# Seven products of quarters in both layers' channel mixers, token sums on GpSimd, and other ring slots ahead of attention

## The reference

```python
def swiglu(h, wg, wu, wd):
    return (jax.nn.silu(h @ wg) * (h @ wu)) @ wd

def block_tail(...):
    ...
    x = x + g1[:, None, :] * rmsnorm(mixed, n_post_mix)
    hf = modulate(rmsnorm(x, n_pre_ffn), sh2, sc2)
    return x + g2[:, None, :] * rmsnorm(swiglu(hf, w_ffn_gate, w_ffn_up, w_ffn_down), n_post_ffn)
```

## Time and profile before

| what | before |
|---|---|
| median of 3 runs | 2259.72 us (2258.64 to 2261.53) |
| the profiled execution's own time | 2261.28 us |
| its span in the trace | 2259.5 us |
| PE busy | 2172.2 us, 96% of the span |
| DVE busy | 1421.0 us, 63% |
| ACT busy | 884.2 us, 39% |
| POOL busy | 107.5 us, 5% |
| mean granted TensorE clock | 0.987 |
| weight loads (raw<-w_main) | 276 of 512 KB, 3.7 us from issue to landing |

### The profile page before, as it was taken

One profiled execution on the slowest core, in us unless ns is written; L12 is line 12 of the kernel. 1 busy time (PEld: TensorE's weight loads), 2 busy tenths in 40 slices (PEclk: granted clock), 3 DMA queues, 4 the chain that ended last, 5 costly groups with the idle time before them and its releaser, 6 DMA issues.

```text
span 2259.5 us, 34079 instructions
## 1 busy us (share of the span) xinstructions
PE 2172.2 (96%) x14296; PEld 2061.5 (91%) x14296; DVE 1421.0 (63%) x2226; ACT 884.2 (39%) x1417; POOL 107.5 (5%) x199
## 2 busy tenths in 40 slices
PE   5999999899999999999979999999999999999997
PEld 3999999899979899999969999999999798999996
DVE  5587765377747543343375777674765557878785
ACT  4644432376334221221265544324763434332332
POOL 1000011010000000000000000001100000000000
PEclk9999999999999999999999999999999999999998
DMA  6333244123335212222204332443233512222223
GB/s 273 98 112 113 88 162 139 64 93 144 115 98 190 102 66 84 75 66 67 97 11 149 112 113 89 160 148 103 87 112 70 180 59 66 76 93 75 94 75 131
DMA packets 61785, 239.92 MB, mean 106 GB/s; under 512 B 7936, under 2 KB 7968, under 8 KB 59200
## 3 DMA queue, kind: packets, MB, share of 16 engines
q1 hardware_dynamic: 41040, 153.12, 20.7%
q0 software_dynamic: 20592, 84.62, 10.7%
HBM read 226.67 MB, written 11.04 MB: 105 GB/s over the span
## 4 chain that ended last, share of the span: by engine, by line
PE 86%; DVE 6%; ACT 3%; DMA 3%; issue 1%; DVEq 1%; ACTq 0%; POOL 0%; SPq 0%; POOLq 0%
PE unit L473 12%; PE unit L474 12%; PE unit L476 12%; PE unit L461 11%; PE unit L462 11%; PE unit L463 11%; PE sc L463 2%; PE sc L462 2%; PE sc L461 2%; DVE junk L1593 2%; DMA raw<-w_main 2%; PE tp L463 2%; PE tp L461 2%; PE tp L462 2%; PE tp L738 1%
## 5 line engine op out<-in xcount | busy, mean ns | idle before, releaser
L473 PE MATMUL unit<-hmh,wh 128*128 128x320 f32 x1728 | 520.9, 309 | 2.0 <-DVE vl L1503 1.2
L474 PE MATMUL unit<-hml,wh 128*128 128x320 f32 x1728 | 520.8, 310 | 0.0
L1493 DVE TENSOR_TENSOR wl<-raw,wh 128x1024 fp32r<-128x1024 f32 x240 | 291.1, 1222 | 258.0 <-ACT wh L1073 253.0
L476 PE MATMUL unit<-hmh,wl 128*128 128x320 f32 x1728 | 394.1, 309 | 0.0
L473 PEld LDWEIGHTS unit<-hmh,wh 128*128 128x128 f32 x1728 | 324.3, 188 | 3.9 <-issue 2.9
L474 PEld LDWEIGHTS unit<-hml,wh 128*128 128x128 f32 x1728 | 324.6, 188 | 1.1
L1073 ACT ACTIVATE wh<-raw 128x1024 fp32r<-128x1024 f32 x240 | 246.8, 1050 | 130.7 <-DMA raw<-w_main 130.4
L476 PEld LDWEIGHTS unit<-hmh,wl 128*128 128x128 f32 x1728 | 289.0, 188 | 0.0
L1593 DVE CUSTOM_DVE_ANT_0 junk<-ada,csb,par 128x1024 f32<-128x1024 f32 x160 | 205.6, 1285 | 23.1 <-DMA ada<-w_ada 2.6
L461 PE MATMUL unit<-wh,hmh 128*128 128x256 f32 (+1 forms) x640 | 201.9, 315 | 16.0 <-DVE nv L1503 8.8
L462 PE MATMUL unit<-wl,hmh 128*128 128x256 f32 (+1 forms) x640 | 200.1, 313 | 0.0
(11 more groups left out here) (436 smaller groups left out, 4210.3 us busy)
## 6 DMA issues: line engine op xcount, KB each, us to landing
raw<-w_main SPq DMA_DIRECT2D x276, 512.0 KB, 3.7
ada<-w_ada POOLq DMA_DIRECT2D x80, 512.0 KB, 4.2
first<-w_first SPq DMA_DIRECT2D x8, 1024.0 KB, 19.0
bias<-biases POOLq DMA_DIRECT2D x32, 192.0 KB, 2.7
x<-x POOLq DMA_DIRECT2D x2, 2560.0 KB, 12.1
x<-x_keep POOLq DMA_DIRECT2D x2, 2560.0 KB, 10.5
bias<-biases POOLq DMA_DIRECT2D x16, 256.0 KB, 3.9
gains<-g_rows POOLq DMA_DIRECT2D x4, 1024.0 KB, 5.4
```

The costliest lines, as they stand in the source:

```text
L473: pe.matmul(u[:, h, 0:n], a[0], xs[h][0], start=f, stop=False)
L474: pe.matmul(u[:, h, 0:n], a[0], xs[h][1], start=False, stop=False)
L476: mm = pe.matmul(u[:, h, 0:n], a[1], xs[h][0], start=False, stop=z)
L1493: dve.tensor_tensor(wl[slot[i]][:, :], raw[slot[i]][:, :], f32(wh[slot[i]][:, :]), ALU.subtract)\
```

## The change

It has these parts.

1. Blocks 2 to 10 of the first layer's channel mixer take seven products too; all conditions on the last layer go, and semaphore counts get an offset per layer. The slabs of the first layer's gate and up are stored in the other order that `seven` wants.
2. With that the first layer gets what only the last had: x is stored to x_keep by tiles and loaded back before the layer's end, the ring has six slots from slab 76 on, block 1 has its two splits less, ACT copies its first down tiles, the gains are loaded late. New is that POOL loads rel, pos and rope again after the last seven products (`constants_of_heads`), and that DVE and ACT wait for it at the second layer's start.
3. t1w, t2w and t4w are made by POOL in both layers (`token_sum`), not by DVE.
4. Since t4 destroys csb, the ada pieces of blocks 0 and 1 fall from 10 to 6, all in block 0. Two more pieces go to the first head after head 0 in each layer, two others to the gates.
5. `TURNED` fixes the slots of slabs 39, 40 and 41 of each layer, and 42 and 43 are held to slots 0 and 1.
6. Small moves: ACT takes the silu of csb one copy earlier; at the first layer's end the split of slab 140 moves from tile 4 to behind the last tile.

```diff
+TURNED = {39: 0, 40: 3, 41: 2, PER_LAYER + 39: 1, PER_LAYER + 40: 2, PER_LAYER + 41: 3}
-HEADS_ADA, LAST_ADA = 15, 32
+HEADS_ADA, LAST_ADA = 17, 32
...
-            may = range(SIX) if i // PER_LAYER == DEPTH - 1 and j >= 4 + W_O + KD else range(2) if NARROW <= j < WIDE else range(2, RING) if NARROW - 2 <= j < NARROW else range(RING) if j < WIDE or LAST <= j < LAST + 4 else range(RING, RING + MORE) if j >= LAST - 2 else range(RING + MORE)
+            may = (TURNED[i],) if i in TURNED else range(SIX) if j >= 4 + W_O + KD else range(2) if NARROW - 4 <= j < NARROW - 2 or NARROW <= j < WIDE else range(2, RING) if NARROW - 2 <= j < NARROW else range(RING) if j < WIDE else range(RING + MORE)
...
                 def gate_up(b):
-                    if l < DEPTH - 1 or b < SEVEN:
+                    if b < SEVEN:
                         for _ in range(4):
                             column()
...
+            def constants_of_heads():
+                for to, of in ((rel[:, :], rel_in), (pos[:, :, :], pos_in), (rope[:, :, :], rope_in)):
+                    g.dma_start(to, of).then_inc(const_in, 16)
...
+            def token_sum(n, a, b, more):
+
+                to = whole_sums[n]
+                g.tensor_tensor(to, a, b, ALU.subtract).then_inc(ts_step, 1)
+                token_steps.add()
+                for other, op in more:
+                    g.wait_ge(ts_step, token_steps.count)
+                    i = g.tensor_tensor(to, to, other, op)
...
-                    modulation(10)
+                    modulation(4)
+                token_sum(0, h12, h11, ((l12, ALU.add), (l11, ALU.subtract)))
+                if l == 0:
+                    modulation(2)
+                g.wait_ge(ts_full, 4 * l + 1)
+                token_sum(1, h22, whole_sums[0], ((l22, ALU.add),))
+                if l == 0:
                     g.wait_ge(ada_done, FIRST_ADA)
+                g.wait_ge(ts_full, 4 * l + 2)
+                token_sum(3, h21, whole_sums[1], ((l21, ALU.add),))
+                last_gate = (l + 1) * SEVENS - 2
+                g.wait_ge(seven_done, 7 * (last_gate + 1))
                 gains_on_all(1)
-                if l == DEPTH - 1:
-
-                    g.wait_ge(seven_done, 7 * (last_gate + 1) + 3)
-                    g.dma_start(x[:, :, :], x_keep).then_inc(x_back, 16)
+                g.wait_ge(seven_done, 7 * (last_gate + 1) + 3)
+                g.dma_start(x[:, :, :], x_keep).then_inc(x_back, 16)
+                if l < DEPTH - 1:
+                    g.wait_ge(seven_done, 7 * (l + 1) * SEVENS)
+                    constants_of_heads()
...
-                        elif n == 0:
-                            sum_of_tokens(0)
-                            sum_of_tokens(1)
-                        else:
+                        elif n:
                             low_of_tokens((3,))
                         if l == 0:
-                            modulation((1, 3)[n] if b == 0 else (2, 2)[n] if b == 1 else 0)
+                            modulation(3 if b == 0 else 0)
...
-                if l == DEPTH - 1:
-                    dve.wait_ge(x_back, (l + 3) * 16)
+                dve.wait_ge(x_back, (2 * l + 3) * 16)
```

More of the change, by code:

```diff
@@ L442, in build @@
         slab_done = []
+        h11, h12, h21, h22 = (f32(hmh[:, k:k + 4, h * HALF:h * HALF + HALF]) for k in (0, 4) for h in range(2))
+        l11, l12, l21, l22 = (f32(hml[:, k:k + 4, h * HALF:h * HALF + HALF]) for k in (0, 4) for h in range(2))
         FIRST_ADA = DEPTH * ADA - 2 * KD - LAST_ADA
@@ L879, in seven @@
                     pe.wait_ge(ws_ready, r + 1)
-                    pe.wait_ge(ts_ready, 2)
+                    pe.wait_ge(ts_ready, 4 * l + 2)
                     if r:
@@ L890, in seven @@
                     pe.wait_ge(w_lo[slot[i + 1]], turn_of[i + 1])
-                    pe.wait_ge(ts_ready, 4)
+                    pe.wait_ge(ts_ready, 4 * l + 4)
                     pe.wait_ge(seven_copied, r + 1)
@@ L977, in modulation @@
                     adas.add()
+            token_steps = Tally()
+            def token_sum(n, a, b, more):
[5 more added lines that the diff above has]
+                    i = g.tensor_tensor(to, to, other, op)
+                    if other is more[-1][0]:
+                        i.then_inc(ts_full, 1)
+                    else:
+                        i.then_inc(ts_step, 1)
+                        token_steps.add()
             for l in range(DEPTH):
@@ L1207, in _ @@
                     U.release(act.activation(y[:, 4, :], u[:, 0, 0:DV], ACT.Copy))
-                    u = U.get()
-                    U.release(act.activation(y[:, 0:4, :], u[:, :, :].rearrange("p a (b n) -> p (a b) n", b=2), ACT.Copy))
                     if h == 0:
@@ L1212, in _ @@
                         act.activation(csb[:, :, :], csb[:, :, :], ACT.Silu).then_inc(cs_ready, 1)
+                    u = U.get()
+                    U.release(act.activation(y[:, 0:4, :], u[:, :, :].rearrange("p a (b n) -> p (a b) n", b=2), ACT.Copy))
                     heads.add()
@@ L1414, in seven_copy @@
                 def seven_copy(r):
+                    r += l * SEVENS
                     act.wait_ge(seven_done, 7 * r + 1)
@@ L1462, in _ @@
                         U.add(TILES)
-                        if l < DEPTH - 1:
-                            split(2)
                 act.activation(flag_a[:, :], epsc[:, :], ACT.Sqrt)
@@ L1478, in _ @@
                         root(x[:, t, :], mix[:, t, :], ss2, rt2, t)
-                    if l == 0 and t in (2, 3, 4):
+                    if l == 0 and t in (2, 3, 5):
                         split()
@@ L1638, in head_norm @@
                 if h == 0 and layer.count:
-                    dve.wait_ge(x_saved, layer.count * 16)
+                    dve.wait_ge(x_saved, layer.count * (TILES + 1) * 16)
                 gain = [par[:, layer.count, GN + h * 2 + c:GN + h * 2 + c + 1] for c in range(2)]
@@ L1790, in _ @@
                         if c < 3 or j == 0:
-                            modulation(1)
+                            modulation(2 if l == 0 and j and c == 1 else 1)
                 dve.drain()
@@ L2149, in main_slabs @@
     gate_up = [np.concatenate([slabs_of(w[:, b * 256:(b + 1) * 256], P)[[i]] for i in range(2) for w in (w_fg, w_fu)]) for b in range(FB)]
-    if last:
-        for b in range(SEVEN, FB):
-            gate_up[b] = gate_up[b][[0, 2, 1, 3]]
+    for b in range(SEVEN, FB):
+        gate_up[b] = gate_up[b][[0, 2, 1, 3]]
     down = [slabs_of(w_fd[b * 256:(b + 1) * 256], 512, 2) for b in range(FB)]
```

123 lines of the change are left out of this document (47 added, 76 removed).

## The result

The changed kernel takes 2233.07 us, median of four runs (2231.71 to 2235.8), against 2260.62 us (2258.64 to 2261.76) of the kernel before on the same chip: a ratio of 0.9882, 95% interval 0.9868 to 0.9897. It is faster by 27.5 us; I had forecast 41, and the measured time lies 3.6 us outside my range. The profiled execution took 2232.49 us, its span is 2230.7.

A forecast was written before the change was run, and what follows sets the result against it. PE, busy for 96% of the span, was taken as the bound. 33.48 + 10.31 - 2.74 = 41.05 us off the profiled 2261.28 gave 2220.2, or 2218.7 us as median, range 2214.5 to 2229.5.

The forecast's parts named there:

- Seven products in layer 1: Blocks 2 to 10 of layer 1 fall from 363.90 to 330.42 us, as in layer 2: 33.48 us less.
- Slots ahead of attention: The two `values` ahead of attention in layer 1 fall from 39.40 to 29.09 us: 10.31 us less.
- The wait of 4.1 us ahead of down(0) in both layers: PE's 4.12 us wait stays in layer 2 and comes to layer 1, whose blocks 0 and 1 take 2.74 us more.
- Ada pieces: Block 0 of layer 1: three pieces ahead of the first multiply instead of one, 4.6 us of cover, cost 0.
- POOL's seven adds: Token sums in both layers: 3 us per add, 21 in all, hidden behind eight columns of PE, cost 0.
- GpSimd holds DVE: Rival, chance 0.11: in layer 1 POOL's adds stop DVE for 10.4 us, 5.8 reach PE, giving 2224.5 us.
- My own sign of being wrong: The forecast is wrong if, among other signs, DVE's ada pieces grow beyond 1.28 us each by more than a third.
- The clock: Waits of a few us may find the lower clock (0.97 and 0.95 in blocks 0 and 1): 3 us either side.
- The head of layer 2: The moved silu and moved split are as in layer 2 or stand where an engine waits: cost 0.
- x comes back late: Rival, chance 0.07: x's load at layer 1's end is 2.8 us late, 2221.5 us; with the tables up to 15.
- the wait only moves: Rival, chance 0.05: ahead of attention in layer 1 the 10.3 us are not gained, giving 2229.0 us.
- a far slower GpSimd: Rival, chance 0.04: PE's second quarter waits for token sums; at 12 us per add 80 us are lost, 2298.5.

The follow-up runs named there:

- experiment 4: The changed kernel with the down pair's second slab split ahead of block 1's last multiply, on ACT and DVE, both layers: 2215.64 us.
- experiment 1: The changed kernel with the seven adds of token sums back on DVE instead of POOL, in both layers: 2224.49 us.
- experiment 6: The changed kernel with ACT waiting for the three tables in layer 1 alone and the split back at t = 4: 2235.29 us.

## Why the prediction was right and wrong

*Seven products in layer 1: right.* 33.47 us for 33.48. *Slots ahead of attention: right* in layer 1 (10.33 for 10.31); slabs 39 and 41 were in time. That layer 2 needed them as well I had not seen; it cost nothing, since the change holds both layers. *The wait of 4.1 us ahead of down(0) in both layers: right*, and for the reason given; experiment 4 took it away.

*Ada pieces: wrong, in "PE needs the unit at 718.38: 4.6 us of cover, cost 0".* I took the first multiply's reader one column too late. In the changed kernel PE stops 14.4 us behind the mixer's start (698.16 after 683.78); put into the trace of before that is 711.4, when the multiply was over at 708.13. So 3.2 us were free, where I reckoned with 10.2 (4.6 after the pieces), and 5.6 us of pieces overdraw them: 2.4 by this, 2.6 measured (experiment 1).

*POOL's seven adds: the price was right, "the sums are hidden behind eight columns of PE: 0" was not.* The sums are ready when ACT comes for them, but they hold DVE. The rival was in the text (GpSimd holds DVE, chance 0.11) with 5.8 us on PE; 7.4 are measured. I worked its size from DVE's rate for the adds, 10.4 us. What counts is the add of POOL that a DVE instruction meets, 2.97 us and not 1.49: the holds sum to 12.5 us in layer 1, 7.4 of them ahead of the first multiply (and to 10.8 in layer 2, where PE waits for none of them). And I let 4.6 us of cover stand against it, which with the right deadline are not there. My own sign of being wrong came true: ada instructions grew from 1.28 to 3.8 us, far beyond a third. The Trainium skill's section "1. Specifications" of "GPSIMD Engine Reference" names just this contention, for DVE instructions with two SBUF inputs; the trace agrees: of the long rows all are such (ada, wl, hidl), and the multiplies `sig<-unit,sig`, with one input in PSUM, stay at 0.82 to 0.88 us beside a running add. I gave the rule a chance of 0.11 where a term was due.

*The clock.* Between the two causes and 82.61 us some 3.5 are left (82.61 - 69.15 - 9.98): the granted clock of the stretch is 0.86 where layer 2 had 0.95 before. In the 11.9 us behind the long wait it is 0.74, which alone makes about 3.1 us. So a wait of 10 us costs about 13. My sum had no term for a clock that falls further than in the rows of before, only 3 us on either side.

*The head of layer 2: wrong, in "the moved silu and the moved split are as in layer 2 or stand where an engine waits: 0".* From the last downs of layer 1 to the end of layer 2's heads the changed kernel takes 2.4 us more than that of before. The moved split stands in front of dst, and the new wait for the tables, for which the sum has no term at all, put the table load behind dst; experiment 6 took away 2.7 us with both.

*x comes back late, the wait only moves, a far slower GpSimd: none of them.* No row of the last downs waits for a load.

The profiled execution gained 28.8 us against 41.05, 12.3 less. What I missed on the dear side sums to 16.9: 10.0 for the wait, 3.5 for the clock, 2.4 for the head of layer 2, and 1.0 in blocks 0 and 1 of layer 2, where down(0) behind the same wait runs at a granted clock of 0.83 instead of 0.89. Against it stand 4.6 us of small gains that I had not counted either: the first column starts 1.8 us earlier (40.55 for 42.34), the attention and second norm of layer 1 are 1.1 shorter, and the stretch ahead of attention in layer 2 is 1.7 shorter. Their causes were not looked for; that they softened the miss by a quarter is luck.

## What to carry to other kernels

Work moved to GpSimd is not free for VectorE: beside it each VectorE instruction with both inputs in SBUF can wait for a whole GpSimd instruction, so ask which of them stand in front of something that TensorE waits for, and compare the hold (up to one GpSimd add for each of them) with what was saved; here 12.5 against 10.4 us. Cover has to be read from the one instruction that stops when the work is late: a deadline taken one column too late turned a wait of 2.6 us into 4.6 us of imagined room, and hid the price of everything behind it. When a version is measured, repair the next wait in the same stretch as well, since a wait of a few us takes some more with it through TensorE's clock (4.1 us were worth some 6.3 in each layer). And look at the rest of the program after a repair: the edits of experiment 6 took 2.7 us away where they stand, and four of the five kernels that have them lost 3 to 7 us elsewhere, for a reason that stays open.

## What the hardware showed beyond that

- GpSimd and VectorE take turns at whole instructions. An add of 1280 holds an ada instruction by 2.5 us, one of 640 by 1.1; GpSimd's own add grows from 2.97 to as much as 3.96 us in return.
- An add of 1280 fp32 elements a partition takes GpSimd 2.97 us, VectorE 1.49: 2.0 times.
- Ahead of the second norm of layer 2, beside four stores of 1024 separate elements, two slabs of 512 KB take 12 to 17 us to land in every trace, where 4.1 is the median of all. In the four traces where they took over 14 us PE waited 3 to 7 us for them. A store of an eighth of the size changed nothing, and the cause is open.
